# A two-layer hybrid trunk on one core: an activation table loaded earlier, and several steps of the first projection and of the second layer moved

## The reference, cut to what matters

```python
def rmsnorm(x, g):
    y = xf * lax.rsqrt(jnp.mean(xf * xf, axis=-1, keepdims=True) + NORM_EPS)
    return (y * g.astype(F32)).astype(x.dtype)

h = x
for layer in range(DEPTH):                      # DEPTH = 2
    hn = rmsnorm(h, mix_norm[layer])
    h = h + (even_mixer if layer % 2 == 0 else odd_mixer)(hn, ...)   # p = hn @ w_in; ...; y @ w_out
    h = h + squared_relu_mlp(rmsnorm(h, mlp_norm[layer]), w_up[layer], w_down[layer])
return rmsnorm(h, final_norm)
```

```python
S = S * w_t[:, :, None, :] - sa[..., None] * b_t[:, :, None, :] + v_t[..., None] * k_t[:, :, None, :]
```

## Time and profile before

| | us |
|---|---|
| median of 3 runs | 1358.56 |
| lowest, highest | 1357.12, 1362.73 |
| the profiled execution, its own time | 1360.57 |
| its span | 1358.4 |
| PE busy | 1300.2 (96%) |
| DVE, ACT, POOL busy | 568.1, 536.7, 659.7 |
| granted PE clock, mean | 0.981 of full |

### The profile page before, as it was taken

The page is one execution under the profiler, slowest core; times in us unless marked ns, Lnnn a source line. Parts: engine busy times, 40 slices in busy tenths (PEclk is TensorE's granted clock), DMA queues, the critical chain, the costliest instruction groups (busy, mean ns, idle before and its releaser), DMA issues.

```text
span 1358.4 us, 18265 instructions
## 1 busy us (share of the span) xinstructions
PE 1300.2 (96%) x6685; PEld 1041.8 (77%) x6685; DVE 568.1 (42%) x913; ACT 536.7 (40%) x880; POOL 659.7 (49%) x810
## 2 busy tenths in 40 slices
PE   5999978999999999999989899899999999999997
PEld 3877756788888888887767677788878888888886
DVE  4438665421221211244689955477531121121233
ACT  5335664341331322435662524753442232231332
POOL 4653224565554555565344534212555555554553
PEclk9999988999999999999989899899999999999999
DMA  9322101333333333333212221000333333333331
GB/s 276 82 77 76 48 16 47 94 93 93 93 93 93 93 93 93 94 92 93 62 48 76 79 62 47 1 2 1 93 93 94 93 93 93 93 93 93 94 91 62
DMA packets 198036, 108.87 MB, mean 80 GB/s; under 512 B 4570, under 2 KB 195280, under 8 KB 197968
## 3 DMA queue, kind: packets, MB, share of 16 engines
q1 hardware_dynamic: 197552, 107.88, 27.8%
q0 software_dynamic: 416, 0.07, 0.0%
HBM read 105.83 MB, written 2.10 MB: 79 GB/s over the span
## 4 chain that ended last, share of the span: by engine, by line
PE 83%; DVE 9%; ACT 4%; issue 2%; DMA 0%; POOL 0%; DVEq 0%; SPq 0%; ACTq 0%
PE ps L904 23%; PE ps L905 23%; PE ps L906 23%; PE ps L891 2%; DVE arena L2346 1%; PE ps L945 1%; PE ps L1305 1%; PE ps L946 1%; PE ps L947 1%; DVE arena L2464 1%; DVE y_mix L2467 1%; DVE relu L2330 1%; PE ps L1062 1%; PE ps L1093 1%; PE ps L1379 1%
## 5 line engine op out<-in xcount | busy, mean ns | idle before, releaser
L810 POOL TENSOR_TENSOR w_lo<-raw_w,w_hi 128x256 fp32r<-128x256 f32 x760 | 617.9, 844 | 589.6 <-ACT w_hi L1458 589.6
L1458 ACT ACTIVATE w_hi<-raw_w 128x1024 fp32r<-128x1024 f32 x190 | 201.1, 1058 | 533.1 <-PE ps L906 422.8
L904 PE MATMUL ps<-hn_hi,w_hi 128*128 128x512 f32 x880 | 357.4, 406 | 2.7 <-POOL w_lo L810 1.8
L906 PE MATMUL ps<-hn_hi,w_lo 128*128 128x512 f32 x880 | 349.4, 397 | 0.0
L905 PE MATMUL ps<-hn_lo,w_hi 128*128 128x512 f32 x880 | 349.2, 397 | 0.0
L904 PE MATMUL ps<-hid_hi,w_hi 128*128 128x512 f32 x576 | 227.6, 395 | 0.0
L906 PE MATMUL ps<-hid_hi,w_lo 128*128 128x512 f32 x576 | 227.5, 395 | 0.0
L905 PE MATMUL ps<-hid_lo,w_hi 128*128 128x512 f32 x576 | 227.5, 395 | 0.0
L904 PEld LDWEIGHTS ps<-hn_hi,w_hi 128*128 128x128 f32 x880 | 166.4, 189 | 49.8 <-issue 8.3
L905 PEld LDWEIGHTS ps<-hn_lo,w_hi 128*128 128x128 f32 x880 | 166.5, 189 | 41.7 <-issue 2.9
L906 PEld LDWEIGHTS ps<-hn_hi,w_lo 128*128 128x128 f32 x880 | 166.0, 189 | 40.7
(11 more groups left out here) (392 smaller groups left out, 1277.0 us busy)
## 6 DMA issues: line engine op xcount, KB each, us to landing
raw_w<-in_w_up SPq DMA_DIRECT2D x64, 512.0 KB, 4.0
raw_w<-in_w_down SPq DMA_DIRECT2D x64, 512.0 KB, 4.0
raw_w<-in_o_w_in SPq DMA_DIRECT2D x27, 512.0 KB, 3.8
raw_w<-in_e_w_in SPq DMA_DIRECT2D x19, 512.0 KB, 3.8
raw_w<-in_e_w_out SPq DMA_DIRECT2D x8, 512.0 KB, 3.4
raw_w<-in_o_w_out SPq DMA_DIRECT2D x8, 512.0 KB, 3.5
rwkv_raw<-in_x SPq DMA_DIRECT2D x4, 512.0 KB, 8.6
out<-arena SPq DMA_DIRECT2D x8, 256.0 KB, 2.9
```

The source lines that it names most:

```text
L810: nc.gpsimd.tensor_tensor(w_lo[:, n % CUT, ks], raw_w[:, n % RING, ks], w_hi[:, n % CUT, ks].bitcast(F32), ALU.subtract).then_inc(w_cut, 1)
L904: mm(o, a_hi, b_hi, start=(k == 0), stop=False)
L906: ins = mm(o, a_lo, b_hi, start=False, stop=(k == KT - 1))
L1458: A(w_hi[:, n % CUT], raw_w[:, n % RING], ACT.Copy).then_inc(w_high, 1)
```

## The change

It has these parts.

1. SP issues the gain row after token tile 0 of x and not before it.
2. ACT runs one square root on a constant (128x1) before the wait for x, so that the table that the square root needs is loaded there.
3. In slot 0 of layer 0, from the third contraction tile on, PE transposes raw x tile k-2 before it waits for operand k. Only tiles 6 and 7 remain behind the slot.
4. In layer 1's front DVE runs `key_part(0)` and `key_part(1)` before `shift(6)`.
5. The substitution is spread thinner: beside the staged tiles 12 to 16 it goes two steps a tile and no longer three, and the five steps left over go between and behind `ssd_front(0)` and `ssd_weights(0)`.
6. `inv_t[0]` moves to the place of `sub_inv`. POOL zeroes it after the low part of slot 24, when `inv_ready` is there, and ACT fills it at j = 24. `inv_d` shrinks to 64 columns a head and lies beside `inv_p`, so that one memset zeroes both, behind slot 26. `t1` and `square_out` move into the room that `inv_t[0]` had.
7. Behind the front ACT starts with `fill_rows(0)`, and PE runs `p_low` and `mats(0,1)` before the four `z_tok`.

```diff
@@ rwkv_chunks
         yield "rv_tok", n
+    yield "p_low", 0
+    yield from products(0, 1)
     for n in range(NT):
         yield "z_tok", n
-    yield "p_low", 0
-    yield from products(0, 1)
     yield from low_merge(0)
@@ tiles
-        inv_d, inv_t0, inv_p = (cut(late, (4 + j) * 1024, 8, P) for j in range(3))
-        inv_t = (inv_t0, cut(stage_t, 0, 8, P))
+        inv_t = (cut(y_t, 3072, 8, P), cut(stage_t, 0, 8, P))
+        inv_dp = cut(late, 4096, 1024)
+        inv_d, inv_p = (cut(late, 4096 + j * 512, 8, HALF) for j in range(2))
@@ sync
-            sp.dma_start(gain_row, dram["mix_norm"][0:1, :].to_broadcast([P, D])).then_inc(gain_in, 16)
...
             load_x(0)
+            sp.dma_start(gain_row, dram["mix_norm"][0:1, :].to_broadcast([P, D])).then_inc(gain_in, 16)
             load_x(1)
@@ gpsimd
+                    if n == base["in", 1] + 24:
+                        pool.wait_ge(S["inv_ready"], 1)
+                        nc.gpsimd.memset(inv_t[0], 0.0).then_inc(S["inv_zero"], 1)
                     if n == base["out", 1] + CUT - 1:
                         full(pool, "rw", 11)
-                        nc.gpsimd.memset(inv_t[0], 0.0).then_inc(S["inv_zero"], 1)
-                        nc.gpsimd.memset(inv_d, 0.0).then_inc(S["inv_zero"], 1)
-                        nc.gpsimd.memset(inv_p, 0.0).then_inc(S["inv_zero"], 1)
+                        nc.gpsimd.memset(inv_dp, 0.0).then_inc(S["inv_zero"], 1)
@@ tensor
+            def turn_x(k):
+                turn(("x", k), [x_tok_in[:, t, k * P:(k + 1) * P] for t in range(NT)])
+            def normed_beside_x(k):
+                if k >= X_LAG:                      # X_LAG = 2
+                    turn_x(k - X_LAG)
+                operand_ready(0)(k)
...
-                        turn(("x", u), [x_tok_in[:, t, u * P:(u + 1) * P] for t in range(NT)])
+                        if u >= KT - X_LAG:
+                            turn_x(u)
@@ scalar
             act.wait_ge(ident_in, 16)
+            A(mv[:, 0, 0:1], eps[:, 0:1], ACT.Sqrt)
             token_root_mean(0)
...
+                if j == 24:
+                    fill_columns(0)
...
-            fill_columns(0)
+            fill_rows(0)
             for t in range(NT):
                 full(act, "rv_tok", t)
             for t in range(NT):
                 drain(v_tok[:, t, :], "rv_tok", t)
-            fill_rows(0)
@@ vector
             take_staged(6)
-            shift(6)
             key_part(0)
             key_part(1)
+            shift(6)
             take_staged(7)
...
             for i in range(12, 17):
                 take_staged(i)
-                substitute(3 * i - 28, 3 * i - 27)
+                substitute(2 * i - 16, 2 * i - 15)
                 conv_staged(i)
-                substitute(3 * i - 27, 3 * i - 25)
+                substitute(2 * i - 15, 2 * i - 14)
...
-            substitute(23, 25)
+            substitute(18, 20)
             ssd_front(0)
-            substitute(25, 26)
+            substitute(20, 22)
             ssd_weights(0)
-            substitute(26, 31)
+            substitute(22, 31)
```

More of the change, by code:

```diff
@@ L293, in rwkv_chunks @@
             yield "y_tok", n
+X_LAG = 2
 STAGE_AT = 13056
@@ L690, in trunk @@
         y_rw = cut(arena, 4 * T, NT, 512)
-        square_out = cut(y_t, 3584, 256)
+        square_out = cut(late, 5632, 256)
         s_rw = cut(arena, tail + 1024, 2, 512)
@@ L694, in trunk @@
         neg_u = cut(arena, tail + 2560, 512)
-        t1 = cut(y_t, 3072, 512)
+        t1 = cut(late, 5120, 512)
         v_tok = cut(rwkv_raw, 8 * (T + 1), 4, T)
@@ L926, in project_in @@
                 close(feature_tile(free(pe, *key), n % CUT, hn_hi, hn_lo, PARTS * n,
-                                   before=operand_ready(3 * layer) if j == 0 else None), *key)
+                                   before=None if j else normed_beside_x if layer == 0 else operand_ready(3)), *key)
             def turn_projected(key, buf):
@@ L1324, in odd @@
                             ins = mm(o[0:HALF, hh * HALF:(hh + 1) * HALF], inv_p[0:HALF, hh, :],
-                                     inv_d[0:HALF, hh, 0:HALF], start=True, stop=True)
+                                     inv_d[0:HALF, hh, :], start=True, stop=True)
                         close(ins, *item)
@@ L1775, in ssm_squares, with fill_columns, fill_rows @@
                            accum_out=gss[:, 2 * n + g:2 * n + g + 1]))
+            def fill_columns(n):
+                if n >= 2:
+                    full(act, "u", n - 2)
+                act.wait_ge(S["inv_ready"], 1)
+                act.wait_ge(S["inv_zero"], (1, 3, 4, 5)[n])
+                for q in range(P // SUB):
+                    rows = slice(q * SUB, (q + 1) * SUB)
+                    ins = A(inv_t[n % 2][rows, :, rows], inv_cols[rows, :, n * 8:n * 8 + 8].rearrange("p c j -> p j c"),
+                            ACT.Copy)
+                ins.then_inc(S["inv_filled"], 1)
+            def fill_rows(n):
+                if n:
+                    full(act, "t_high", n - 1, 1)
+                act.wait_ge(S["inv_zero"], 2)
+                for q in range(P // SUB):
+                    rows, own = slice(q * SUB, (q + 1) * SUB), slice(q % 2 * SUB, (q % 2 + 1) * SUB)
+                    ins = A(inv_d[rows, :, own], inv_rows[rows, :, n * 8:n * 8 + 8].rearrange("p c j -> p j c"), ACT.Copy)
+                ins.then_inc(S["inv_filled"], 1)
             for j, (_, key) in enumerate(ODD_SLOTS):
@@ L1848, in turned @@
                 drain(bb_tok[:, n % 2, :], "rb_tok", n)
-            def fill_blocks(n, src, dst, zeroed):
-                act.wait_ge(S["inv_ready"], 1)
-                act.wait_ge(S["inv_zero"], zeroed)
-                for q in range(P // SUB):
-                    rows = slice(q * SUB, (q + 1) * SUB)
-                    ins = A(dst[rows, :, rows], src[rows, :, n * 8:n * 8 + 8].rearrange("p c j -> p j c"), ACT.Copy)
-                ins.then_inc(S["inv_filled"], 1)
-            def fill_columns(n):
-                if n >= 2:
-                    full(act, "u", n - 2)
-                fill_blocks(n, inv_cols, inv_t[n % 2], (1, 4, 5, 6)[n])
-            def fill_rows(n):
-                if n:
-                    full(act, "t_high", n - 1, 1)
-                fill_blocks(n, inv_rows, inv_d, 2)
             def high_merge(n):
@@ L2597, in keep_pairs @@
                 if n == 0:
-                    dve.wait_ge(S["inv_zero"], 3)
+                    dve.wait_ge(S["inv_zero"], 2)
                 o = heads8(full(dve, "p_low", n))
```

5 lines of the change are left out of this document (2 added, 3 removed).

## The result

The changed kernel takes 1341.3 us (median of 4 runs, 1339.96 to 1341.81); the kernel before, run beside it, 1360.64 (4 runs, 1357.12 to 1363.01). The ratio is 0.9867, 95% interval 0.9845 to 0.9889. The forecast was 1340. The profiled execution took 1340.78 us by its own time, with a span of 1338.8 against 1358.4. The granted clock was 0.985 on average, against 0.981.

A forecast was written before the change was run, and what follows sets the result against it. PE was taken as the bound, busy 1300.2 us of a 1358.4 span. Six terms, 1.2 + 1.2 + 6.7 + 3.4 + 2.0 + 3.9 = 18.4 us, off the 1358.56 median gave 1340 us, range 1334 to 1349.

The forecast's parts named there:

- The start: First loads before slot 0: gain row after tile 0 and early square-root table bring the last tile's taking 1.2 us earlier.
- Raw transposes: Layer 0, slot 0: transposes placed among PE's matmuls leave less behind the slot, 1.2 us earlier.
- Key parts: Layer 1's front: two key parts in DVE's gap before `shift(6)` remove PE's wait and low clock at `sub(0)`, 6.7 us.
- Thinner substitution: Layer 1's front from 706 us: four fewer DVE steps before the last convolution's taps, priced without POOL contention, 3.4 us.
- the clock behind it: PE from 772 to 777 us: the half-rate clock behind the second silu stall no longer falls, 2.0 us.
- The recurrence: End of layer 1's front up to `u(0)`: one ACT fill goes and PE works during ACT's drains, 3.9 us.
- The thinning brings nothing: Rival: in layer 1's front ACT's chain keeps the silu stalls and low clock; 1345.5 us, chance 0.17.
- the key parts don't move: Rival: the key parts wait for something near 683 us anyway, leaving start and recurrence alone; 1352 us, chance 0.07.
- The deeper win: Rival: removed substitution steps are worth 1.7 us each, with a higher clock in the recurrence; 1335 us, chance 0.11.
- The slower one: Rival: POOL waits for a late `inv_ready` and PE starves at slot 25; 1366 us when 40 us late, chance 0.03.

The follow-up runs named there:

- e6: Changed kernel with all raw transposes behind slot 0 again (`X_LAG = KT`): 1340.28 us, ratio 0.9862.
- e7: Changed kernel with the recurrence's old order, without filling `inv_t[0]` in slot 24: 1345.02 us, ratio 0.9892.
- e4: Kernel before with the thinner substitution alone: 1349.32 us, ratio 0.9917.
- e3: Kernel before with the first two key parts moved ahead of `shift(6)` alone: 1354.29 us, ratio 0.9956.
- e10: Changed kernel with 48 extra products on DVE between the substitution's last step and the inverse: 1362.26 us, ratio 1.0018.
- e8: Changed kernel with `ssd_back(0)`, `ssd_front(1)` and `ssd_weights(1)` ahead of staged tile 17 on DVE: 1333.84 us, ratio 0.9815.
- e11: Changed kernel with the gain row loaded behind token tile 1 instead of tile 0: 1339.7 us, ratio 0.9845.
- e1: Kernel before with only the first transfers reordered, the gain row issued after token tile 0: 1356.21 us, ratio 0.998.
- e12: Changed kernel with the product of token tile 3 done twice at the start: 1341.95 us, ratio 0.9877.

## Why the prediction was right, point by point

- *The start, 1.2.* Right in its direction and too small: it measured 2.7 in this pair and 2.0 in the means of four and six traces. The step that failed is "the bytes ahead of it are the same as before", so that the last tile lands at 14.4 as before. It landed 1.3 earlier in this pair and 0.7 earlier in the mean (13.9, then 13.2), and it varies by more than that within one order (13.12 to 14.33 with the row first, 12.89 to 14.64 behind tile 0). The rate with the row first is low in all five traces; why it is, no run shows. The other part of the term was right: ACT stood 1.5 behind the last landing, and that went. That either edit alone would do the same is wrong: the order does it all (13.05), the table a little over half (14.3).
- *Raw transposes, 1.2.* 1.27 in the trace and 1.28 against e6, but 0.7 in the mean of seven traces: five of them begin slot 0 at the low clock, and a slot that PE bounds pays for it. The sum had no term for this; that the pair hit 1.2 is luck. The 0.83 of wait stayed. The two terms together put the stacks at 29.8 in the mean of five traces against 32.4 in the mean of four, so 2.6, where 2.4 was forecast and this pair shows 4.0.
- *Key parts, 6.7.* The lead rose by 6.7; two key parts took 5.5 us where about 5.8 was worked out, the gap left is 1.83, `sub(0)` has neither wait nor low clock. Alone it brings the same in its own place and 5.5 up to the first `y_diag`, in part because the clock still falls behind the silu stalls.
- *Thinner substitution, 3.4, and the clock behind it, 2.0.* Together 7.3 in place of 5.4. From slot 10 on, `take_staged(16)` and the transposes behind it gained 4.7 us, 1.17 a step and not 0.85: in the new trace instructions of 252 to 256 elements take 0.42 or 0.83 to 0.96, so the steps do meet POOL's work, and a price without contention was too low. The Trainium skill, page "SBUF — State Buffer", section "SBUF: two separate sides", says that whichever of the two instructions starts first holds a shared port for its whole length and blocks the other; I had concluded from it that the steps removed cost nothing of it. The measurement decides against this conclusion, not against the port. The clock gave the other 2.66 (no wait of PE stands in that stretch in either trace): in the changed kernel it is granted in full from 757.7 to 776.9, where the earlier trace rows have 0.85 and the earlier trace rows 0.50 behind the longer stall.
- *The recurrence, 3.9.* 4.3 in this pair of traces, 3.1 against e7's, 3.9 in the mean over fourteen. The size was right; a single pair would have said either, and a match to a tenth is luck.
- *What the sum left out.* The clock in unchanged code: +1.4 in layer 0, then -0.6, -1.9 and -1.6. Two of the losses have a place: a wait of 2.32 at the second `y_diag` (2.04 before) and one of 1.59 at `u(0)`, each with a low clock behind it that lasts longer than in the kernel before. The first, in the windows view, the kernel before and then after:
```profile
807.00:812.60 5.60, 5.60 (x27) 4.79 (x28) 4.57 (x6) 0.00 (x0) 2.83 (x3) 0.70 0.27 84
```
```profile
788.40:794.00 5.60, 5.60 (x23) 5.05 (x24) 3.51 (x5) 0.00 (x0) 2.55 (x3) 0.58 0.28 94
```
  The terms that were too small (1.5 for the start, 1.9 for substitution and clock, 0.4 for this pair's recurrence) outweigh these net losses of 2.6, so the six terms' 18.4 stands against 19.6 of span; the kernel before ran at 1360.6 beside the changed one and not at 1358.6. The total is closer than its parts deserve, and in part that is luck.
- *The rivals.* "The thinning brings nothing" is refuted by e4 (7.8 in its stretch), "the key parts don't move" by e3. The deeper win came about in its mechanism, in part (1.17 a step, not 1.7), though not in its total. The slower one was named with the wrong place: from 6.1 us of further lateness on, and through DVE's SSD steps, not through POOL. Its price was nearly right: with DVE's idle time down by 8.3 and 24.5 us more work (e10), in sum 32.8, where 33 was to bring the total back to 1358.6, it measured 1362.3.

The 0.6 lost ahead of slot 8 and the differences of the totals below 3 us stay open: single runs of one kernel differ by more.

## What to carry to other kernels

Where a helper engine is full, count both its idle gap behind an in-order wait and what could fill it: work whose operands are ready goes ahead of the wait, for here that order gave 6.7 us in its place, and once more 5.8 (e8). Price a stall with what follows it: the waits of 2.3 to 4.5 us cost another 1.8 to 3.4 here in PE's clock. Read a term of 1 or 2 us from several traces: the start measured 2.7 in one pair and 2.0 in the mean, the raw transposes 1.3 and 0.7. When work is pushed back behind the critical stretch, look for the first instruction that waits behind it in the same queue, not at the idle time of the engine that it is meant to serve.

## What was not expected of the hardware

- With a row broadcast to 128 partitions (512 KB) as the first large load, the rate from 3.5 to 5.0 us is 109 to 260 GB/s (five traces); with a plain tile of the same size ahead of it, 246 to 377 (eight traces). With the row behind two tiles the rate dips to 242 to 274 from 6.5 to 8.0 (e11 alone). That the row itself is slow wherever it stands is not shown: behind one tile e1 has 288 to 303.
- The granted clock behind the same stall in the same code isn't fixed. Behind the same two waits of layer 0 (1.9 and 2.2 us) it was 0.66 in the changed kernel and 1.00 in e12; behind the wait of 2.32 at the second `y_diag` the next step took 20.50 in the changed kernel and 18.89 in e6; unchanged layer 0 took 604.69 to 607.87 us in the fourteen traces. A term of this size can't be read from a single trace.
- Both table loads take 1.28 us, and the silu at 837.09 begins 0.01 behind the end of the load at 835.80. The Trainium skill, page "ScalarE: Activation LUTs", section "What ACT_TABLE_LOAD costs", gives about 1283 ns for the load and another 1380 ns for a drain; the trace agrees with the first, and the second does not show as time between the load and the next instruction.
